# Cached key pages laid over 32 partitions and turned in blocks by VectorE, in place of whole pages over 128 partitions turned by TensorE

## The reference

```python
h = x @ w_in                                   # 1024 -> 5200 columns, split into 11 groups
o_a = HGRN2 recurrence (4 heads, 128 x 128 state), RMSNorm, SiLU gate
q, k, v  (8 heads x 64, partial rotary);  qi, ki, wi  (indexer: 16 heads x 64, one key)
scores = sum_h relu(qi_h . ki) * wi_h          # over cached and new tokens
sel    = top_k(scores, 256)                    # 128 for the prompt
p      = softmax(q . k[sel] / 8);  o_b = p . v[sel]
y = LayerNorm(ALPHA * x + [o_a ; o_b] @ w_out)
```

## Time and profile before

| | |
|---|---|
| median of 3 runs | 743.45 us (743.27 to 748.41) |
| profiled execution | 744.93 us, span 743.2 us |
| the loop, from the first key transposes to the last logits | 258.06 to 530.08 us |
| TensorE busy in the span | 704.7 us (95%) |
| VectorE, ScalarE, GpSimd busy | 463.7, 245.1, 203.1 us |
| bytes moved by DMA | 114.12 MB |

### The profile page before, as it was taken

The page is one execution under the profiler, slowest core; times in us unless marked ns, Lnnn a source line. Parts: engine busy times, 40 slices in busy tenths (PEclk is TensorE's granted clock), DMA queues, the critical chain, the costliest instruction groups (busy, mean ns, idle before and its releaser), DMA issues.

```text
span 743.2 us, 13976 instructions
## 1 busy us (share of the span) xinstructions
PE 704.7 (95%) x4842; PEld 409.2 (55%) x4842; DVE 463.7 (62%) x976; ACT 245.1 (33%) x559; POOL 203.1 (27%) x330
## 2 busy tenths in 40 slices
PE   5887999999999999999999999999999999789994
PEld 4434444444544555567765556777557777653441
DVE  0204279999999874555556464645577786684435
ACT  3114720114666422222222232222564446420000
POOL 1730004115798632222222222222100002640000
PEclk9999999999999999999999999999999999989998
DMA  9910053133130087798887889977220008301511
GB/s 274 312 57 1 2 175 106 67 104 130 50 129 1 2 277 250 255 348 283 276 277 256 256 242 294 348 246 251 71 72 1 2 5 298 111 1 41 185 43 42
DMA packets 60005, 114.12 MB, mean 154 GB/s; under 512 B 7217, under 2 KB 20610, under 8 KB 59938
## 3 DMA queue, kind: packets, MB, share of 16 engines
q1 hardware_dynamic: 31970, 54.57, 23.3%
q0 software_dynamic: 12608, 40.67, 16.6%
q10 hardware_dynamic: 15360, 18.02, 7.4%
HBM read 106.01 MB, written 7.23 MB: 152 GB/s over the span
## 4 chain that ended last, share of the span: by engine, by line
PE 84%; DVE 4%; DMA 4%; issue 2%; ACT 2%; ACTq 1%; POOL 1%; SPq 1%; DVEq 0%; POOLq 0%
PE banks L561 18%; PE banks L821 12%; PE banks L1088 7%; PE banks L735 7%; PE banks L807 7%; PE banks L783 4%; PE banks L752 4%; DMA arena<-in_cache_k 3%; PE banks L896 2%; PE banks L927 2%; PE banks L699 2%; PE banks L772 2%; PE banks L645 2%; DMA arena<-in_x_prompt 1%; PE banks L909 1%
## 5 line engine op out<-in xcount | busy, mean ns | idle before, releaser
L561 PE MATMUL banks<-wbuf,xT 128*128 128x512 f32 (+1 forms) x448 | 147.8, 524 | 4.3 <-issue 4.1
L336 POOL DMA_DIRECT2D arena<-in_cache_v x128 | 70.2, 549 | 199.4 <-issue 199.4
L561 PEld LDWEIGHTS banks<-wbuf,xT 128*128 128x128 f32 (+1 forms) x448 | 65.3, 172 | 80.8 <-issue 75.4
L821 PE MATMUL banks<-wbuf,xT 128*128 128x512 f32 (+1 forms) x288 | 104.7, 530 | 0.0
L1533 DVE TENSOR_REDUCE small<-banks 128x1 f32<-128x512 f32 x32 | 22.1, 691 | 93.3 <-PE banks L752 93.3
L1514 DVE MAX8 small<-arena 64x8 f32<-64x2112 f32 x32 | 75.1, 2348 | 1.3
L1516 DVE MATCH_REPLACE8 arena<-small,arena 64x2112 f32<-64x2112 f32 x32 | 74.7, 2334 | 0.0
L735 PE MATMUL banks<-ident,arena 128*128 128x128 f32 x512 | 68.1, 276 | 0.9 <-DMA arena<-in_cache_k 0.9
L735 PEld LDWEIGHTS banks<-ident,arena 128*128 128x128 f32 x512 | 56.4, 141 | 22.4 <-issue 18.1
L807 PE MATMUL banks<-xT,arena 128*128 128x288 f32 x256 | 67.4, 406 | 0.0
L1277 ACT COPY wbuf<-banks 128x512 f32<-128x512 f32 x64 | 37.3, 582 | 70.7 <-PE banks L735 70.7
(11 more groups left out here) (251 smaller groups left out, 1028.6 us busy)
## 6 DMA issues: line engine op xcount, KB each, us to landing
arena<-in_cache_k SPq DMA_DIRECT2D x128, 256.0 KB, 3.4
arena<-in_cache_v POOLq DMA_DIRECT2D x128, 256.0 KB, 3.9
wbuf<-in_w_in ACTq DMA_DIRECT2D x6, 2048.0 KB, 10.4
wbuf<-in_w_in SPq DMA_DIRECT2D x2, 2048.0 KB, 15.0
arena<-in_w_in ACTq DMA_DIRECT2D x8, 512.0 KB, 6.2
arena<-in_x_prompt SPq DMA_DIRECT2D x4, 512.0 KB, 4.7
wbuf<-in_w_out SPq DMA_DIRECT2D x1, 2048.0 KB, 8.0
xT<-in_w_out SPq DMA_DIRECT2D x1, 2048.0 KB, 13.6
```

Of the source, the lines that this page charges most:

```text
L336: e.dma_start(buf[n % 2][:, i, :], cache[bass.ds(pg, 1), 0].rearrange("a p h d -> p (a h d)")).then_inc(arrived[n % 2], 16)
L561: mm = pe.matmul(psum[a * NS:a * NS + ROWS[t], n % PB, 0:w // split], xT[:, c, t * P:t * P + ROWS[t]], wbuf[:, WB[g], c, a * w // split:(a ...
L821: mm = pe.matmul(psum[a * NS:a * NS + ROWS[t], bank, 0:512 // split], xT[:, c, t * P:t * P + ROWS[t]], wbuf[:, WB[g], c, a * 512 // split: ...
```

## The change

A page of keys goes to 32 partitions, four pages to 128: partition `32 i + p` holds tokens `p`, `32 + p`, `64 + p` and `96 + p` of page `i`, each a row of 2 KB. VectorE turns the buffer in blocks of 32 x 32 with two instructions of 128 x 1024, which leaves on partition `32 i + c` feature `c` of each of 16 blocks of 32 features, tokens along the row. `qdiag` holds the queries of a sequence so that for each block the 32 columns (4 pages by 8 queries) are zero except on the 32 partitions of their own page. One matmul of 128 columns thus takes one block of features of four pages at once. The result has a row for each head pair, page and query, and two times 128 columns (the two heads of a pair), where it had 512 columns.

Since a row now covers a page and not four, `negmax` reduces 128 columns for two heads, turns that, takes the minimum over the pages, and turns it back; `shares` does the like with the sums. `probs` and `pT` have 256 columns where they had 512, and `probs_out` moves from VectorE to ScalarE. `values` comes after `logits` in TensorE's order. The bias is laid out once by eight DMAs (`masks`), the queries by eight more and a transpose (`qst`, `q32`). ScalarE makes `qdiag` of a sequence with four copies (`queries_apart_by_page`), for two sequences ahead of the loop and for the others in iterations 8, 12, ..., 28, and issues key pages 2 and 3 of each iteration from 2 on. SyncE issues pages 0 and 1, and all weights, which come in pieces.

```diff
-                    page_loads(sp, cache_k, k_buf, k_in, n)
+        def key_pages(e, n, which):
+            for i in which:
+                pg = e.value_load(pages[0:1, 4 * n + i:4 * n + i + 1], min_val=0, max_val=NPAGES - 1)
+                e.dma_start(k_buf[n % 2][32 * i:32 * i + 32].rearrange("p (t n) -> p t n", t=4),
+                            cache_k[bass.ds(pg, 1), 0].rearrange("a (t p) h d -> p (a t) (h d)", t=4)).then_inc(k_in[n % 2], 16)
...
+                for n in range(2, NG):
+                    sp.wait_ge(kg_ok, 2 * (n - 1))
+                    key_pages(sp, n, range(2))
...
                 def logits(n):
                     s, g = n // 4, n % 4
-                    pe.wait_ge(kg_dve, 2 * n + 2)
-                    pe.wait_ge(kg_act, 2 * n + 2)
+                    if n == 0:
+                        pe.wait_ge(masks_got, 8 * 16)
+                        pe.wait_ge(diag_ok, 1)
                     if n >= 2:
-                        pe.wait_ge(ex, q_no(n - 2) + 1)
+                        pe.wait_ge(ex, ex_no(n - 2))
+                    if g == 0:
+                        pe.wait_ge(qdiag_ok, 4 * (s + 1))
+                    bank = psum[:, SB0 + n % 2, 0:2 * P]
+                    page = masks[:, (4 * (s // 4) + g) * P:(4 * (s // 4) + g + 1) * P]
+                    pe.matmul(bank, pick4[:, s % 4 * P:(s % 4 + 1) * P], page.unsqueeze(1).to_broadcast([P, 2, P]),
+                              start=True, stop=False, skip_group_check=True)
+                    pe.wait_ge(kg_ok, 2 * n + 2)
+                    for u in range(2):
+                        for e in range(2):
+                            for j in range(4):
+                                d = 4 * j + 2 * u + e
+                                mm = pe.matmul(bank[32 * j:32 * j + 32, u * P:(u + 1) * P],
+                                               qdiag[s % 2][:, d].rearrange("p b q -> p (b q)"), kg_v[n % 2][:, d],
+                                               start=False, stop=(e == 1), skip_group_check=True)
...
+                def queries_apart_by_page(s):
+                    c = s % 4 * NNEW
+                    if s >= 2:
+                        act.wait_ge(qk, 5 * (s - 1))
+                    for b in range(4):
+                        r = slice(32 * b, 32 * b + 32)
+                        nc.scalar.copy(qdiag[s % 2][r, :, b, :], q32_v[r, s // 4, :, c:c + NNEW]).then_inc(qdiag_ok, 1)
...
                 for n in range(NG + 1):      
...
+                    if n:
+                        probs_out(n - 1)
+                    if n and n % 4 == 0:
+                        probs_new_out(n // 4 - 1)
+                    if n % 4 == 0 and 4 < n < NG:
+                        queries_apart_by_page(n // 4)
+                    if n + 2 < NG:
+                        act.wait_ge(kg_ok, 2 * (n + 1))
+                        key_pages(act, n + 2, range(2, 4))
...
+                def turn_keys(n):
+                    dve.wait_ge(k_in[n % 2], 64 * (n // 2) + 64)
+                    if n >= 2:
                         dve.wait_ge(qk, q_no(n - 2) + 1)
+                    for a in range(2):
+                        w = slice(1024 * a, 1024 * a + 1024)
+                        nc.vector.transpose(kg[n % 2][:, w], k_buf[n % 2][:, w]).then_inc(kg_ok, 1)
...
+                    me.link(nc.vector.tensor_reduce(mark[:, 0:2], psum[:, SB0 + n % 2, 0:2 * P].rearrange("p (u n) -> p u n", u=2),
+                                                    AX.X, ALU.max, negate=True))
+                    me.link(nc.vector.transpose(marks_t, mark))
+                    over_pages(ALU.min, low, marks_t)
+                    nc.vector.transpose(tops[s % 2][:, g], low).then_inc(mx, 1)
```

More of the change, by code:

```diff
@@ L292, in hybrid_step @@
         v_buf = [carve(4 * W2).rearrange("p (g n) -> p g n", n=W2) for _ in range(2)]
+        masks = carve(W2).bitcast(BF16)
+        mark, marks_t, low = (carve(32) for _ in range(3))
+        row_sums = [carve(32) for _ in range(2)]
+        qst = arena[:, 23040:23040 + 2 * W2]
+        assert qst.shape == q32.shape and SCORES + LS + NS <= 23040
+        pick4 = runs[:, 0:256].bitcast(BF16)
+        tops = [runs[:, 256 + a * P:256 + (a + 1) * P].rearrange("p (g n) -> p g n", g=4) for a in range(2)]
+        sums_t = runs[:, 512:544]
+        qbd = ga[:, NT]
+        qdiag = [ga[:, 2 + a].rearrange("p (e b q) -> p e b q", e=16, b=4) for a in range(2)]
+        q32_v = q32.rearrange("p (t e c) -> p t e c", t=2, e=16)
         seq = [small[:, a:a + 32] for a in (0, 160)]
@@ L748, in logits @@
-                    bank = psum[:, SB0 + n % 2, :]
-                    pe.matmul(bank, pick[:, s * P:(s + 1) * P], bias_s[:, g * 512:(g + 1) * 512], start=True, stop=False,
-                              skip_group_check=True)
-                    for j in range(4):
-                        mm = pe.matmul(bank[32 * j:32 * j + 32, :], queries(s, j), kg[n % 2][:, j, :],
-                                       start=False, stop=(j == 3), skip_group_check=True)
+                        pe.wait_ge(ex, ex_no(n - 2))
@@ L855, in _ @@
                         turn_probs_new(n // 4 - 1)
-                    if not last:
-                        turn_keys(n, 1)
-                        unit(n, 1)
-                    else:
-                        token_tile(GA_, 0, everything[4:])
-                    if n == 1:
-                        pe.wait_ge(banks_ok, 4)
-                    if n:
-                        values(n - 1)
-                    if n and n % 4 == 0:
-                        values_new(n // 4 - 1)
                     if not last:
@@ L1613, in strike @@
                         nc.vector.match_replace(SP[b], best[:, b, :], SP[b], TAKEN).then_inc(topk, 1)
+                new_queries()
                 dve.wait_ge(pacc, 3 * HI)
+                for a in range(4):
+                    ins = nc.vector.tensor_copy(pick4[:, a * P:(a + 1) * P].rearrange("p (c i q) -> p c i q", c=4, i=4),
+                                                ident[:].rearrange("p (i s q) -> p s i q", i=4, s=4)[:, a].unsqueeze(1)
+                                                .to_broadcast([P, 4, 4, NNEW]))
+                    if a < 3:
+                        me.add(ins)
+                me.wait()
+                ins.then_inc(diag_ok, 1)
+                me.add(nc.vector.memset(mark, 0.0))
+                me.add(nc.vector.memset(row_sums[0], 0.0))
+                me.add(nc.vector.memset(row_sums[1], 0.0))
+                me.wait()
                 dve.wait_ge(roped, ROPED_Q[NT - 1])
```

198 lines of the change are left out of this document (113 added, 85 removed).

## The result

The changed kernel took 770.31 us in the median of four runs (768.92 to 772.47), beside 744.38 us for the kernel before on the same chip: a ratio of 1.034, 95% interval 1.029 to 1.039. It is slower, where I forecast 699 us. The profiled execution took 768.92 us, span 767.2 us.

The account below looks back on a forecast made before the run. TensorE's work was taken as the bound, transfers the next limit. TensorE 192.8, query waits 11.4, late pages 6.0 and start 1.0 made 211.2 against 256.67 us, 45.5 less than before: 699 us, range 687 to 712.

Parts of the forecast that it names:

- Transfers: Page loads in the loop: bytes unchanged at 69.6 MB, 341 GB/s needed, 0.2 us an iteration for late pages, 6 us.
- signs of being wrong: Profile after: block transposes above 1.46 us, TensorE waiting mainly for DMA, or a loop clock below 1.00.
- the transfers are the bound: Rival for the loop: DMA rate limits it, 717 us at 305 GB/s, 729 at 290, 735 with slower key packets; chance 0.21.
- far side: Transfers rival's extreme: key packets 1.7 times as long, 8.9 us an iteration, 755 us, slower than before; chance 0.03.
- What leaves TensorE: Loop on TensorE: key transposes, two probability transposes and part of the bias go, 63.9 us in 30 iterations, leaving 192.8.
- VectorE: Loop: block transposes at 1.13 us, 24.9 us per four iterations against TensorE's 25.7; nearly all busy, barely off the path.
- rival of dear transposes: Block transposes on VectorE at 2.27 us each put it on the path, 8.6 us an iteration, 753 us; chance 0.07.
- The wait that the change adds: TensorE waits 1.9 us for ScalarE's query copies in six iterations: 11.4 us, range 5 to 18.
- The clock: Rival: clock falls to 0.66 for 5 us in each of six new waits, costing 10 us, 709 us; chance 0.04.
- The start: Before the loop: turning queries and first keys, copies and memsets on VectorE add 1.0 us, range 0 to +4.
- After the loop: After the loop: the same units and copies follow as before, 0 us.

Follow-up runs that it names:

- both waits taken out: Changed kernel with pages on every fourth partition, queries two iterations earlier, and two sigmoids after the loop ahead of `probs_out(31)`: 705.98 us, ratio 0.956.

## Why the prediction was wrong

- **"Transfers"** is the step that failed. The sum had 6.0 us for it, 0.2 an iteration for late pages; the waits that are not for the queries measured 53.3 (64.6 - 11.3). I wrote "feasible, but only just" on the ground that 394 GB/s had been reached and that "four pages together cover all partitions". A rate is reached by transfers of a kind, and the change replaced that kind. In the new kind the full engines carried 289 GB/s in the program and 303 by themselves beside value pages. The price was 47.2 us more of waits than the 17.4 forecast, and 12.9 us of a slower clock in them (205.7 - 192.8): together the 60.1 us by which the stage missed its 210.2. Two of my signs of being wrong stood in the profile: TensorE waited mainly for DMA, and the clock of the stage was 0.90.
- **The rival "the transfers are the bound"** had the mechanism and gave it 0.24 with its far side. It took too little in three ways: it counted the queues over 8 us where an iteration had 8.56 (over 8.56 its own sum gives 744 and 765 us in place of 735 and 755); it charged the key packets alone, while the value packets slowed as well (45 to 56 engine-us a MB) and the weights landed in 17.1 us instead of 6.2; and it took TensorE to run at full clock beside the waits. By rate, 69.6 MB at 289 GB/s are 241 us; at the measured mean of 255 they are 273. I cut 275 to 545 us into 27 windows of 10 us. In 22 of them the share was 1.02 or more, at a mean of 268 GB/s and not 289, which makes 260 us; the other five had shares from 0.51 to 0.90, the emptiest of them (405 to 415) right behind the stall of 13.59 us that ended at 400.97. The lowest rate at a full share, 223 GB/s, stood from 355 to 365, where SyncE's queue carried 1671 packets of 1.0 KB in the mean (weights among them) at 81 engine-us a MB, for 1.8 KB and 59 from 290 to 340. How much of that is the packets' length was not tried. The far side came nearest in time, 755, but not by its own sum: it had the keys' packets 1.7 times as long, where engine time a MB is 60 against 45 with whole pages, 1.3 times, and the values' 56 against 47.
- The Trainium skill ("SBUF — State Buffer", "Door 1: The DMA port swizzle") gives 189 GB/s for 32 partitions and 328 for all. These runs agree: 212 and 340, and 64 partitions in the low half (23.0 us) no better than two queues on 32 each there (22.0). The ports that it names as the reason are in no trace; the runs show the rates. Its section "Can I just issue two DMAs to hit both halves?" says no: two at once measured 6% over a single one. Here the measurement differs and decides: 15.3 us for two queues in two halves, 22.0 for both in the low half. I used the first rule as a rival of 0.03, with a chance far too small.
- **What leaves TensorE**: right. 5.84 us for a token iteration, logits 0.90 (forecast 1.00), transposes and bias as forecast (0.22, and 0.20 for 0.21).
- **VectorE**: near. A block transpose of 128x1024 took 1.22 us, not 1.13, the page maximum 1.24, not 1.07 (269.19 to 270.43). It was busy in 65% of the stage (176.95 of 270.30 us), not in about 95%; even where the stage took 217.87 us, with every fourth partition and both waits taken out, it was 81%. TensorE waited 1.6 us for it, behind late keys, so VectorE didn't bind the loop, and the rival of dear transposes is out. The Trainium skill's rule of one element per cycle per lane ("Vector Engine (DVE) Microarchitecture Reference", section 3.8) fits this: 1.19 ns a column beside the 1.11 of the earlier trace rows, no second pass.
- **The wait that the change adds**: right at 11.3 us (forecast 11.4) in six waits of up to 2.0, and removed by moving the copies; but in the changed kernel its removal was worth nothing while the DMA was full.
- **The clock**: the rival of 0.04 looked for it in the query waits and had 10 us. It fell behind the stalls for DMA (0.50 from 350 to 360 us). Of the query waits, the one of 1.82 us before 371.52 left the logits at 1.08 us, the one of 2.00 before 415.66 was followed by 1.70.
- **The start**: +2.9 for +1.0, inside its 0 to 4.
- **After the loop**, put at 0, cost 7.4 us. `probs_out(31)` now stands on ScalarE ahead of the sigmoids and waits for transposes behind a 7.1 us unit; the chain comes out at TensorE's first transposed probabilities of the prompt, and the values of iteration 31 also lie later. Up to that point 4.5 us are lost. Behind it the granted clock was 0.52 for 5.4 us and 0.84 for the next 5, where before it was 1.00, and the other 2.9 us lie from there on.

```profile
547.49 7.13 PE L873 MATMUL banks<-wbuf,xT 128*128 128x512 f32 x16
554.46 0.38 PE L824 MATMUL banks<-ident,arena 128*128 128x128 f32 x2
...
569.57 0.33 PE L963 MATMUL banks<-ident,wbuf 128*128 128x128 f32 x1 [3.58 <-ACT wbuf L1408]
```

With the sigmoids ahead, that idle time is gone and the stretch from the last bias matmul to the end is 216.0 us (486.2 to 702.2), 5.7 less than with every fourth partition alone (497.0 to 718.7) and 1.2 more than before.

With these three faults mended the ratio 0.956 stands for 711 us on the basis of 743.45, 12 above the 699. In that kernel's profile (703.89 us) the stage takes 217.87 us (268.37 to 486.24) with TensorE busy in 195.69 at a mean clock of 0.96; the forecast had 210.2 and 192.8. TensorE still waits 13.9 us for weights and 3.2 for values there. Another order of issue doesn't return them: with the weights on ScalarE's queue they were in time, keys and values were late instead, and the time was the same (706.71). What would bring the rest stays open; deeper buffers for the weights were not tried.

## What to carry to other kernels

Before a transfer is reshaped, ask into which half of the partitions it goes, not only how many bytes it has: a rate that the profile shows holds for the shape that reached it. A layout that needs few partitions can take every fourth one, which here kept the rate of whole pages (345 GB/s, for 334). When the DMA share is at 1.0, lower the DMA's own time first: here moving the weights to another queue or the query copies forward moved the wait and not the time, and two other orders of the key pages cost some 12 us more.

## What the runs showed of the hardware

- DMA engines count as fully busy (share 1.00 to 1.05) both at 212 and at 394 GB/s; the share alone doesn't tell how much a loop can still move.
- Transfers into one half of the partitions slow the others beside them: values, untouched, went from 45 to 56 engine-us a MB, and by themselves quarters on one queue beside values had 264 GB/s where whole pages had 353.
- 64 partitions across the middle (32 to 95) are as fast as two queues in two halves: 14.9 and 15.3 us for 4 MB; 0 to 63 take 23.0. Two queues that take the same half in turn gain nothing: 209 GB/s for quarters 0, 2 and 1, 3, where 0, 1 and 2, 3 have 304 and one queue has 212.
- Matmuls whose moving operand is read in runs of 4 columns (every fourth partition) took 1.08 us in the group, as those with runs of 32: no price.
- A VectorE block transpose of 128x1024 float32 takes 1.22 us, one of 128x32 takes 0.21.
